# TensorE's steps of a beat placed ahead of the products of the beat's picks

## The chip, the cores and the metric

One core of a Trainium2 chip. The time is the device time of one execution in microseconds. The kernel before took 3504.87 us in the median of three runs (3503.13 to 3510.0).

## What is computed

One inference step of a single decoder layer, for a prompt of 1024 rows and eight sample sequences of four rows each behind 1024 cached positions, all in float32:

```python
h = rmsnorm(x, norm1_g)
p = h @ w_in                              # conv 512 | rwkv 1408 | attention 1152 columns
x = x + concat[conv_mixer(p), rwkv_mixer(p), sb_attention(q, k, v)] @ w_out
x = x + peer(rmsnorm(x, norm2_g))
y = rmsnorm(x, final_g)
```

`sb_attention` is a causal attention whose weights are the exponential of a log-sigmoid plus a running sum over later keys (stick-breaking). `rwkv_mixer` has a recurrence over the rows, done here in chunks of 64. `peer` is the costly part: for each row and each of 8 heads it scores 128 + 128 keys, takes the 16 best sums of pairs and with them 16 of 16384 experts, and then

```python
act = gelu(einsum('thkd,td->thk', u_tab[e], xb))
out = einsum('thk,thkd->td', gate * act, v_tab[e])
```

so every row fetches 8 x 16 rows of `u` and as many of `v`, 1024 floats each.

## The kernel before

The program has stages (`project`, `scan_rwkv`, `finish_rwkv`) and then `peer`, which begins near 600 us and holds all that the change touches. Rows are worked in nine blocks of 128 (`NBLK`; the ninth holds the 32 sample rows). A block has 8 turns, one for each head (`PH`; the ninth has 2), and a turn has 16 picks (`TOPK`), done in 8 groups of two (`GROUPS`, `GP`). A group is a *beat*; a full block has 64 of them, 512 in all with steps beside the picks, and 16 more in the ninth block.

The life of pick m:

- POOL (L1336) gathers, by the expert numbers of the turn, one row of `u` and `v` for each of the 128 partitions, 1 MB, into slot m mod 7 of `uv_ring` (`RING` is 7). Before it, it waits for `uv_free` to reach m - 6: the products of pick m - 7 are done.
- VectorE (L1769) waits for the gather and multiplies the `u` half with `h2`, summing to one number per row (`hidden`).
- ScalarE takes the gelu of both picks of the group (L1985), multiplies by the gate (L1989) and writes a diagonal matrix (`diag`, L1996; six of them, `DIAGS`).
- TensorE waits for `diag_done` and multiplies the diagonal with the `v` half, in four products that add to the banks `Y` (L2464), and raises `uv_free`.

Behind the picks of a group each engine does its part of the beat's other work. On VectorE this is gates, a piece of the choice of experts two turns ahead (`choose`, on odd beats), and `beside`. On ScalarE it is `exps` and `beside`. On TensorE it was the scores of a head three turns ahead (`score`, in the fifth beat of a turn), the spread of the final gain (`final_gain`, once a block) and `beside`. On POOL it is the fetch of a page of cached keys or values, now and then.

`beside(b, n)` is the same frame on every engine (`beats`): by the block and the number of the beat it calls what is due there, by tables written out by hand (`scans`, `finishes`, `early_seq`, `late_att`, and the constants `CLOSE`, `SPREAD`, `TURN`, `LATE`, `EARLY`):

- `attend`: attention of a later block in units of four tiles. Unit u has its scores in beat 2u (TensorE, L2371), logits in 2u + 2 (VectorE, L1672), softplus in 2u + 2 (ScalarE) and 2u + 3 (VectorE, L1684), sums over later keys in 2u + 3 (TensorE, L2385 and L2387), differences in 2u + 5 (VectorE), weights in 2u + 6 (ScalarE, L1935), values in 2u + 6 (TensorE, L2402). Scores wait for the logits of the unit before.
- `scan`: one chunk of the recurrence in 16 beats. Step n of TensorE (L2144) needs what VectorE (L1509 to L1526) or ScalarE (L1857 to L1863) makes in step n out of TensorE's step n - 1. There are 13 such chunks in the loop.
- `sample`: the attention of one sample sequence over its cached pages, in 22 beats, page by page (L2096, L2121); `scan_sample`: the recurrence of the samples, in the seventh block; `finish`: the group norm of the recurrence (L2351, L2354).
- closing of the next block: eight products with rows of `w_out` in beats 24 to 31 (`close_y`, L2056), residual and norm in beats 33 to 38 (`close_gain`, L2077, and `close_turn`, L2085, on TensorE).

Each engine runs its own program in order; only semaphores join them. SP loads what `beside` reads, waiting for counters that TensorE's steps raise. `beside` on TensorE waits for results of VectorE and ScalarE by semaphores as, in a scan:

```python
if n == 6:
    evicted("vr2")
    each("r3", lambda i, r: mm(lo(0)[r, i, :], p2[r, PR + i, :], rb[r, i, :]))
```

where `evicted("vr2")` waits until VectorE has written `r2` of this chunk, which it does in its own step 6.

Of the kernel before, what the change touches and what calls it, by code (L numbers as in the profile page):

```python
# [943 lines left out]
def peer(nc, io, sb):  # L944
# [11 lines left out]
    last = lambda b: b == NBLK - 1  # L956
    rows_of = lambda b: NS if last(b) else P
    GROUPS = TOPK // GP
# [76 lines left out]
    with ExitStack() as ctx:  # L1035
# [125 lines left out]
        def beats(b, n, attend, sample, scan, scan_sample, finish):  # L1161

            for block, c, first, rate in scans(b):
                for step in range(rate * (n - first), rate * (n - first) + rate):
                    if step in range(16):
                        scan(block, c, step)
            if b == S_TURN and n - S_SCAN in range(0, 2 * S_STEPS, 2):
                scan_sample((n - S_SCAN) // 2)
            for block, first in finishes(b):
                if n - first in range(5):  # L1170
                    finish(block, n - first)
            if b == 0:
                attend(1, n)
            if b and b + 1 < ATTENDED:
                attend(b + 1, n + BEATS - LATE)
            if early_seq(b) is not None:
                sample(early_seq(b), n - EARLY)
            if late_seq(b) is not None:
                sample(late_seq(b), n - LATE)
            if late_att(b) is not None:  # L1180
                attend(late_att(b), n - LATE)
# [824 lines left out]
        def _(pe):  # L2006
            def score(t):
                b, h = divmod(t, PH)
                if h == 0:
                    pe.wait_ge(KA.sem, KA.at("t1", b))  # L2010
                if t:
                    pe.wait_ge(C.sem, C.at("left1", t - 1))
                for c in range(DC):
                    if last(b):
                        for g in range(GR):
                            mine, head = slice(g * NS, (g + 1) * NS), h * GR + g
                            ins = nc.tensor.matmul(scores[mine, :], h2t[:, c, mine], wk[:, c, head * HN:(head + 1) * HN],
                                                   start=c == 0, stop=c == DC - 1)
                    else:
                        ins = nc.tensor.matmul(scores[:, :], h2t[:, c, :], wk[:, c, h * HN:(h + 1) * HN],  # L2020
                                               start=c == 0, stop=c == DC - 1)
                ins.then_inc(score_done, 1)

            def close_y(b, n):

                c = CLOSED_IN[n] if b else n
                if n == 0:
                    if b == 0:
                        for k in range(2):
                            pe.wait_ge(sb.wk_kept[k], PH * 2)  # L2030
                    if 0 < b < ATTENDED:
                        pe.wait_ge(logit_done, unit_at(b + 1, 0))
                        pe.wait_ge(diff_done, unit_at(b + 1, 0))
                    pe.wait_ge(mix_in, 16 * (b + 1 + (GR - 1) * last(b)))
                    if b >= 2:
                        pe.wait_ge(y_ready, b - 1)
                    if b:
                        pe.wait_ge(KA.sem, KA.at("t1", b - 1))
                if c >= DC - PA:
                    if last(b):  # L2040
                        pe.wait_ge(copied, GR)
                    else:
                        pe.wait_ge(out_kept, b + 1)
                if CT <= c < CT + PR:
                    if b:
                        pe.wait_ge(FV.sem, FV.at("gated", b - FRONT))
                    else:
                        pe.wait_ge(first_in, 16)
                recurrent = s_mixed if last(b) else ykept[:, b % 2, :, :]
                left = mixb[:, c, :] if c < CT else recurrent[:, c - CT, :] if c < CT + PR else att[:, c - (CT + PR), :]  # L2050
                if b == 0 and c in (0, len(STREAMED)):
                    pe.wait_ge(wo_in[c != 0], 16)
                if b and c in STREAMED:
                    pe.wait_ge(streamed, 16 * ((b - 1) * len(STREAMED) + c + 1))
                for k in range(2):
                    ins = nc.tensor.matmul(CB(b)[k][:, :], left[:, :], wo_of(b, c)[:, k * 512:(k + 1) * 512], start=n == 0, stop=n == DC - 1)  # L2056
                ins.then_inc(wo_used, 1)

            def final_gain(b):

                if b + 2 < ATTENDED:
                    pe.wait_ge(logit_done, unit_at(b + 3, 0))
                    pe.wait_ge(diff_done, unit_at(b + 3, 0))
                if b + 1 < NBLK and early_seq(b + 1) is not None:
                    pe.wait_ge(SV.sem, SV.at("diff", early_seq(b + 1)))
                pe.wait_ge(KA.sem, KA.at("t1", min(b + 1, NBLK - 1)))
                pe.wait_ge(gain_in, 16)
                for c in range(DC):
                    ins = nc.tensor.matmul(B[c // 4][:, c % 4 * P:(c % 4 + 1) * P], ident[HT:HT + DC, HT + c:HT + c + 1].to_broadcast([DC, P]), gain3,
                                           start=True, stop=True)  # L2070
                ins.then_inc(gain_spread, 1)

            def close_gain(b):

                pe.wait_ge(KV.sem, KV.at("x1", b))
                for c in range(DC):
                    ins = nc.tensor.matmul(B[c // 4][:, c % 4 * P:(c % 4 + 1) * P], ident[0:DC, c:c + 1].to_broadcast([DC, P]), gain2,  # L2077
                                           start=True, stop=True)
                KE.did(ins, "gain")

            def close_turn(b):

                pe.wait_ge(KV.sem, KV.at("h2", b))
                for c in range(DC):
                    ins = nc.tensor.transpose(B[c // 4][:, c % 4 * P:(c % 4 + 1) * P], h2[:, b % 2, c * P:(c + 1) * P], ident[:, :])  # L2085
                KE.did(ins, "turn")
# [328 lines left out]
            def beside(b, n):  # L2415

                beats(b, n, attend, sample, scan, scan_sample, finish)
                if n - CLOSE in range(DC):
                    close_y(b + 1, n - CLOSE)
                if n == SPREAD:  # L2420
                    close_gain(b + 1)
                if n == TURN:
                    close_turn(b + 1)
# [25 lines left out]
            for t in range(TURNS):  # L2449
                b, h = divmod(t, PH)  # L2450
                if h == 0 and b:
                    pe.wait_ge(summed, 4 * b)
                for q in range(GROUPS):
                    for k in range(GP):
                        m = at_group(t, q) * GP + k
                        begin, end = h == 0 and q == 0 and k == 0, t == last_turn(b) and m + 1 == after(t)
                        pe.wait_ge(diag_done, m + 1)
                        if last(b):
                            for j in range(2):
                                ins = nc.tensor.matmul(Y[j][0:NS, :], diag[:, m % DIAGS, 0:NS],  # L2460
                                                       v_row(m, slice(0, P), slice(j * 512, (j + 1) * 512)), start=begin, stop=end)
                        else:
                            for r, j in ((0, 0), (1, 0), (0, 1), (1, 1)):
                                ins = nc.tensor.matmul(Y[r][rows[j], :], diag[rows[r], m % DIAGS, :],  # L2464
                                                       v_row(m, rows[r], slice(j * 512, (j + 1) * 512)), start=begin, stop=end)
                        ins.then_inc(uv_free, 1)
                    if scored(t, q) < TURNS:
                        score(scored(t, q))
                    if b and (h, q) == SPREAD_FINAL[last(b)]:
                        final_gain(b - 1)  # L2470
                    if not last(b):
                        beside(b, h * GROUPS + q)
            pe.wait_ge(y_ready, NBLK - 1)
            final_gain(NBLK - 1)

# [169 lines left out]
```

## Time and profile before

| | |
|---|---|
| median of three runs | 3504.87 us |
| the profiled execution | 3511.46 us |
| its span, first to last instruction | 3509.3 us |
| TensorE products busy | 2804.1 us, 80% |
| VectorE busy | 2522.2 us, 72% |
| ScalarE busy | 1435.5 us, 41% |
| POOL busy | 1371.8 us, 39% |
| mean granted clock of TensorE | 0.874 of full speed |

A busy time is a sum over instructions. The products' ends are modelled and overlap; so TensorE at 80% isn't at its peak. The DMA engines have a row of their own: the mean busy share of sixteen engines, where neighbouring packets may overlap a little, so that 1.01 means full. In the timeline rows below the columns are start, duration, engine, line, operation, result and operands, count, and in brackets the idle time ahead with what ended it.

### The profile page before, as it was taken

How to read it: one execution, taken by the hardware profiler on the slowest of the kernel's cores; microseconds unless marked ns; L12 is line 12 of the kernel's file. 1: busy time of each engine (PE TensorE's matmuls, PEld its weight loads, DVE VectorE, ACT ScalarE, POOL GpSimd, SP SyncE). 2: the span in 40 equal slices, each digit the busy share in tenths (PEclk: the TensorE clock that was granted, in tenths of full speed). 3: DMA queues.
4: the chain of work that ended last, by engine and by line, in shares of the span. 5: the costliest groups of instructions: out<-in, count | busy, mean ns of one | idle time of the engine just before them, and what ended most of it. 6: DMA issues, size and time to landing. Idle time of an engine off the chain costs nothing.

```text
span 3509.3 us, 53126 instructions
## 1 busy us (share of the span) xinstructions
PE 2804.1 (80%) x19302; PEld 1383.5 (39%) x19302; DVE 2522.2 (72%) x5894; ACT 1435.5 (41%) x3859; POOL 1371.8 (39%) x1199
## 2 busy tenths in 40 slices
PE   8999977777778767976797779787878787777657
PEld 4555565434344324432443334334433344323211
DVE  2477333878877877788778877887788777776774
ACT  2121122535533553356335633574357433333332
POOL 0000000443454345434543454345444545454452
PEclk9999988988879888889888888898989888878879
DMA  3122343999999999999999999999999999999998
GB/s 99 40 58 82 107 144 130 403 415 401 410 413 414 395 419 415 404 403 418 416 405 408 415 415 405 396 418 416 403 406 412 417 414 410 401 416 399 409 419 343
DMA packets 248373, 1237.82 MB, mean 353 GB/s; under 512 B 62816, under 2 KB 90384, under 8 KB 112560
## 3 DMA queue, kind: packets, MB, share of 16 engines
q0 software_dynamic: 160256, 1132.54, 79.0%
q1 hardware_dynamic: 87856, 101.90, 8.6%
q8 instruction: 152, 2.49, 0.3%
q14 instruction: 109, 0.89, 0.1%
HBM read 1210.82 MB, written 23.53 MB: 352 GB/s over the span
## 4 chain that ended last, share of the span: by engine, by line
DMA 30%; PE 22%; DVE 20%; ACT 7%; issue 5%; POOL 1%; ACTq 0%; SPq 0%; DVEq 0%; POOLq 0%
DMA uv_ring<-in_peer_uv,expert 30%; PE peer_y L2464 11%; DVE uv_ring L1769 9%; PE peer_s L2020 3%; PE beside L2056 2%; PE scan L2144 2%; ACT diag L1996 1%; ACT L1985 1%; DVE same L1380 1%; DVE same L1382 1%; DVE pick L1384 1%; POOL uv_ring L1336 1%; ACT weights L1989 1%; ACT gelu L1985 1%; ACT L1941 1%
## 5 line engine op out<-in xcount | busy, mean ns | idle before, releaser
L1336 POOL DMA_INDIRECT uv_ring<-in_peer_uv,expert x1056 | 1223.6, 1159 | 1631.3 <-PE peer_y L2464 1282.4
L2464 PE MATMUL peer_y<-uv_ring,diag 64*64 64x512 f32 x8192 | 1250.3, 735 | 574.8 <-ACT diag L1996 541.9
L1769 DVE CUSTOM_DVE_ANT_0 uv_ring<-uv_ring,p_h 128x1024 f32<-128x1024 f32 x1056 | 1270.3, 1222 | 469.7 <-DMA uv_ring<-in_peer_uv,expert 463.5
L2464 PEld LDWEIGHTS peer_y<-uv_ring,diag 64*64 64x64 f32 x8192 | 307.9, 153 | 1181.6 <-ACT diag L1996 795.5
L1985 ACT ACTIVATE gelu<-hidden 128x2 f32<-128x2 f32 x528 | 107.4, 203 | 1420.6 <-DVE hidden L1769 1419.4
L594 PE MATMUL proj<-mix,w_in_tile 128*128 128x512 f32 x672 | 296.7, 600 | 0.0
L1996 ACT ACTIVATE diag<-ident_halves,weights 128x64 f32<-128x64 f32 x1024 | 292.5, 332 | 0.0
L1989 ACT ACTIVATE weights<-gelu,p_gate 128x1 f32<-128x1 f32 x1056 | 254.1, 287 | 50.5 <-ACT gelu L1985 1.5
L2020 PE MATMUL peer_s<-wk,p_h2t 128*128 128x256 f32 x1024 | 252.4, 402 | 4.0 <-DVE cand L1361 4.0
L2020 PEld LDWEIGHTS peer_s<-wk,p_h2t 128*128 128x128 f32 x1024 | 199.9, 201 | 96.4 <-issue 46.2
L1985 ACT ACT_TABLE_LOAD x172 | 220.7, 1283 | 3.0
L594 PEld LDWEIGHTS proj<-mix,w_in_tile 128*128 128x128 f32 x672 | 127.3, 192 | 153.1 <-issue 151.2
L671 POOL COPY v_c<-prc 128x192 f32<-128x192 f32 x2 | 0.7, 338 | 353.8 <-POOLq L129 353.8
L2371 PE MATMUL beside<-att_units,pages_ring 64*128 64x128 f32 x432 | 82.4, 312 | 17.4 <-DMA pages_ring<-scratch_k_tiles 6.8
L273 ACT ACTIVATE prc<-proj 128x512 f32<-128x512 f32 x15 | 9.0, 598 | 202.8 <-PE proj_tails L594 202.8
L418 DVE TENSOR_TENSOR prc<-prc 128x1088 f32<-128x1088 f32 x11 | 14.2, 1290 | 105.1 <-ACT prc L278 105.1
L1941 ACT ACT_TABLE_LOAD x69 | 88.5, 1283 | 1.2
L2371 PEld LDWEIGHTS beside<-att_units,pages_ring 64*128 64x128 f32 x432 | 60.2, 198 | 69.0 <-issue 52.7
L1769 DVE DVE_READ_ACCUMULATOR2_ANT hidden<- 128x1 f32 x1056 | 86.0, 81 | 0.0
L1790 ACT ACT_TABLE_LOAD x65 | 83.4, 1283 | 1.1
L1318 POOL DMA_INDIRECT pages_ring<-in_cache_v,page_rows x64 | 70.9, 1108 | 19.5 <-issue 17.1
L1318 POOL DMA_INDIRECT pages_ring<-in_cache_k,page_rows x64 | 70.6, 1103 | 19.5 <-issue 19.5
(453 smaller groups left out, 3746.3 us busy)
## 6 DMA issues: line engine op xcount, KB each, us to landing
uv_ring<-in_peer_uv,expert POOLq DMA_INDIRECT x1056
w_in_tile<-in_w_in SPq DMA_DIRECT2D x24, 512.0 KB, 3.3
w_out_rows<-in_w_out SPq DMA_DIRECT2D x24, 512.0 KB
uv_ring<-in_w_query SPq DMA_DIRECT2D x8, 1024.0 KB, 7.0
scan_in<-scratch_scan_in SPq DMA_DIRECT2D x15, 480.0 KB, 8.5
pages_ring<-scratch_k_tiles SPq DMA_DIRECT2D x36, 192.0 KB, 12.5
pages_ring<-out_v_new SPq DMA_DIRECT2D x36, 192.0 KB, 11.4
p_x<-in_x_rows SPq DMA_DIRECT2D x9, 512.0 KB, 8.7
```

What stands on the lines that cost most here:

```text
L594: last = nc.tensor.matmul(out, w[:, i % 3, c, :], h[:, c, lo:lo + size], start=c == 0, stop=c == DC - 1)
L1318: pool.indirect_dma_start(out=page[:, slot_of[what], :], out_offset=None, in_=io["cache_v" if kind else "cache_k"], in_offset=bass.Indirec ...
L1336: pool.indirect_dma_start(out=uv_row(m), out_offset=None, in_=io["peer_uv"], in_offset=bass.IndirectOffsetOnAxis(ap=expert[:, t % 4, k:k + ...
L1769: nc.vector.tensor_tensor_reduce(out=u_row(m), in0=u_row(m), in1=h2[:, b % 2, :], scale=1.0, scalar=0.0, op0=ALU.mult, op1=ALU.add, accum_ ...
L1790: nc.scalar.activation(expo[:, :], top[:, :], ACT.Exp, bias=neg[:, 0:1], accum_out=esum[:, 0:1]).then_inc(exps_done, 1)
L1941: nc.scalar.preload_act_table_set("natural_log_exp_and_others")
L1985: nc.scalar.activation(gel[:, g % 2, :], hid[:, g % 2, :], ACT.Gelu_apprx_tanh).then_inc(gelu_done, 1)
L1989: nc.scalar.activation(wgt[:, g % 2, k:k + 1], gel[:, g % 2, k:k + 1], ACT.Copy, scale=gate[:, t % 4, q * GP + k:q * GP + k + 1]).then_inc ...
L1996: nc.scalar.activation(diag[:, m % DIAGS, 0:n], eye[:, 0:n], ACT.Copy, scale=wgt[:, g % 2, k:k + 1]).then_inc(diag_done, 1)
L2020: ins = nc.tensor.matmul(scores[:, :], h2t[:, c, :], wk[:, c, h * HN:(h + 1) * HN], start=c == 0, stop=c == DC - 1)
L2371: ins = nc.tensor.matmul(B[0][:, i * P:(i + 1) * P], page[rows[e], k_slot(kt), h // 2 * P:(h // 2 + 1) * P], q_block[rows[e], h // 2, :], ...
L2464: ins = nc.tensor.matmul(Y[r][rows[j], :], diag[rows[r], m % DIAGS, :], v_row(m, rows[r], slice(j * 512, (j + 1) * 512)), start=begin, sto ...
```

## The change

In each beat of the first eight blocks TensorE calls `beside` ahead of the two picks' products instead of behind them and behind `score` and `final_gain`. The other engines' programs, all waits and all data stay as they are.

```diff
@@ -2451,6 +2451,8 @@
                 if h == 0 and b:
                     pe.wait_ge(summed, 4 * b)
                 for q in range(GROUPS):
+                    if not last(b):
+                        beside(b, h * GROUPS + q)
                     for k in range(GP):
                         m = at_group(t, q) * GP + k
                         begin, end = h == 0 and q == 0 and k == 0, t == last_turn(b) and m + 1 == after(t)
@@ -2468,8 +2470,6 @@
                         score(scored(t, q))
                     if b and (h, q) == SPREAD_FINAL[last(b)]:
                         final_gain(b - 1)
-                    if not last(b):
-                        beside(b, h * GROUPS + q)
             pe.wait_ge(y_ready, NBLK - 1)
             final_gain(NBLK - 1)
```

## Rows read from the trace of the kernel before

**Rows 1.** The page: DMA share in 40 slices, and the two large queues.

```profile
DMA  3122343999999999999999999999999999999998
...
q0 software_dynamic: 160256, 1132.54, 79.0%
q1 hardware_dynamic: 87856, 101.90, 8.6%
```

**Rows 2.** Stretches (busy by engine, clock, DMA share, GB/s), and the products' group.

```profile
644.00:3417.00 2773.00, 2163.08 (x16265) 1034.53 (x16268) 2167.84 (x5323) 1262.02 (x3460) 1320.84 (x1142) 0.86 1.01 410
1430.00:1450.00 20.00, 18.00 (x219) 11.86 (x219) 14.87 (x35) 8.01 (x23) 9.02 (x8) 0.98 0.93 356
1462.00:1484.00 22.00, 22.00 (x157) 10.28 (x160) 15.09 (x38) 5.19 (x22) 8.37 (x8) 1.00 1.01 419
...
L2464 PE MATMUL peer_y<-uv_ring,diag 64*64 64x512 f32 x8112 | 1237.2, 734 | 567.2 <-ACT diag L1996 534.3 <-DVE p_x L1407 31.6
```

**Rows 3.** The chain that ended last, by line.

```profile
DMA uv_ring<-in_peer_uv,expert 30%; PE peer_y L2464 11%; DVE uv_ring L1769 9%; PE peer_s L2020 3%; PE beside L2056 2%; PE scan L2144 2%; ACT diag L1996 1%; ACT L1985 1%; DVE same L1380 1%; DVE same L1382 1%; DVE pick L1384 1%; POOL uv_ring L1336 1%; ACT weights L1989 1%; ACT gelu L1985 1%; ACT L1941 1%
```

**Rows 4.** Waits: who waited for whom, us, times, longest.

```profile
POOL uv_ring L1336 <- PE peer_y L2464: 1282.4, 563, 8.1
...
PE peer_y L2464 <- ACT diag L1996: 541.9, 286, 6.7
DVE uv_ring L1769 <- DMA uv_ring<-in_peer_uv,expert: 463.5, 406, 3.6
...
ACT scan_y L1857 <- PE scan L2144: 28.0, 11, 3.1
```

**Rows 5.** The gathers: issue on POOL (ns, min/median/max) and landing.

```profile
L1336 POOL DMA_INDIRECT uv_ring<-in_peer_uv,expert x1056: 932/945/2000, 607.1 to 3484.6; - x176
...
DMA to landing us min/median/max: 4.9/7.0/12.5
```

**Rows 6.** Timeline 1350 to 1357 us: a scan step fed by VectorE, odd beat.

```profile
1351.34 1.95 PE L2464 MATMUL peer_y<-uv_ring,diag 64*64 64x512 f32 x16
...
1353.73 1.40 DVE L1526 TENSOR_TENSOR ra<-scan,p_ident 64x64 f32<-64x64 f32 x6
...
1355.19 0.56 PE L2144 MATMUL scan<-ra,p 64*64 64x64 f32 x12 [1.90 <-DVE ra L1526]
...
1355.68 0.84 PE L2096 MATMUL beside<-q_diag,pages_ring 128*128 128x8 f32 x6
```

**Rows 7.** Timeline 1370 to 1376 us: a scan step fed by ScalarE.

```profile
1372.02 1.95 PE L2464 MATMUL peer_y<-uv_ring,diag 64*64 64x512 f32 x16 [1.90 <-ACT diag L1996]
1372.11 0.31 ACT L1857 ACTIVATE p<-scan 128x192 f32<-128x192 f32 x1
...
1373.79 0.53 PE L2144 MATMUL scan<-p,xl 64*64 64x64 f32 x12
1374.24 0.83 PE L2096 MATMUL beside<-q_diag,pages_ring 128*128 128x8 f32 x6
```

**Rows 8.** Timeline 1578 to 1587 us: attention, an even beat.

```profile
1581.95 1.95 PE L2464 MATMUL peer_y<-uv_ring,diag 64*64 64x512 f32 x16 [0.42 <-ACT diag L1996]
...
1583.45 0.63 ACT L1935 ACTIVATE att_units<-att_units 128x512 f32<-128x512 f32 x1
1583.83 1.47 PE L2371 MATMUL beside<-att_units,pages_ring 64*128 64x128 f32 x8
...
1585.23 0.66 PE L2402 MATMUL beside<-att_units,pages_ring 128*64 128x128 f32 x8
```

**Rows 9.** Timeline 1595 to 1602 us: attention, an odd beat.

```profile
1597.62 1.95 PE L2464 MATMUL peer_y<-uv_ring,diag 64*64 64x512 f32 x16
...
1598.81 0.68 DVE L1684 SCALAR_TENSOR_TENSOR att_units<-att_units 128x512 f32<-128x512 f32 x1
...
1599.55 1.12 PE L2385 MATMUL beside<-att_units,s_tri 128*128 128x512 f32 x2
1600.52 1.02 PE L2387 MATMUL beside<-att_units,s_ones 128*128 128x512 f32 x2
```

## The prediction

> **What bounds the kernel now.** I read the slices of the page first, then the stretches, the chain, the waits, and last the order of time around single beats. The slices show the DMA engines at nine tenths from the moment the expert stage begins (about 620 us) to the end, and nearly all of what they move comes through the gathers of POOL's queue: 1132.54 MB against 101.90 MB [rows 1]. The stretches are sharper than the tenths: over 644 to 3417 us the DMA share is 1.01 at 410 GB/s, while TensorE is busy 2163 of 2773 us and VectorE 2168 [rows 2]. So the stage lasts as long as its bytes need, and the change moves no byte. A hole in the DMA is rare: 1430 to 1450 us, where the share is 0.93 and 20 us moved at 356 GB/s, is one, around a beat in which VectorE waited for TensorE; the stretch 1462 to 1484 us, in which closing products and picks alternate, is full (1.01) [rows 2]. The chain agrees: 30% of the span is a gather in flight, 11% are the products of the picks [rows 3].
>
> The waits show how close the rest follows. The ring has seven slots, so POOL may issue the gather of pick m only when the products of pick m - 7 are done; POOL waited 1282 us for just that, 563 times. VectorE waited for a gather at 406 of 1056 dots, 463.5 us in all. TensorE waited 541.9 us for a diagonal [rows 4]. It is one closed loop: gather, dot, gelu and diagonal, products, next gather; 2773 us for 8112 / 8 = 1014 picks [rows 2] is 2.73 us a pick, so one turn of the loop takes 7 x 2.73 = 19.1 us, 3.5 beats of 5.47 us.
>
> **The cushion.** A gather issue takes POOL 0.945 us, and a gather lands 7.0 us after it in the median, 4.9 us at least [rows 5]. The 2.1 us between are queueing behind other gathers. That is the cushion: products that end later by less than it leave the DMA engines full. A pick that has landed and waits for VectorE adds to it: at 650 of the 1056 dots VectorE did not wait for the gather.
>
> **The change, part by part.** Nothing is removed or added: the same instructions, waits and bytes. Between the products of beat n - 1 and those of beat n TensorE now does the steps of beat n where it did those of beat n - 1. TensorE's amount of work between two groups of products is the same, so that costs nothing by itself. Score and final_gain keep their place directly behind the products. No DMA is issued by TensorE. SP's and POOL's orders stay; their loads and page fetches that wait for TensorE's steps (wo_used, z_done, k_used, v_used, "state") are released one group of products earlier or, where the step itself waits, later by what is counted below. I cost that at nothing: those loads are asked for several beats ahead, and POOL stands waiting for products anyway; without that cover a page (about one gather issue, 0.945 us) would come on top at 128 page fetches.
>
> What it does add is exposure to waits. VectorE and ScalarE still do their part of beat n behind their share of the picks of beat n. Many steps of TensorE need what those two make in the same beat. Until now TensorE waited for it with the products already done; now the products of beat n are queued behind that wait, and behind them uv_free, the diagonals (six deep) and POOL. Four kinds, each from one beat:
>
> Scan step fed by VectorE on an odd beat. VectorE's choice of the next experts stands ahead of its step, which finishes at 1353.73 + 1.40 = 1355.13; TensorE's steps then take until about 1356.5; the products (1.95 us) would end near 1358.5 and ended at 1353.3: 5.2 us later [rows 6].
>
> Scan step fed by ScalarE. The copy ends at 1372.42, TensorE's steps take 1.3 us, products would end at 1375.7 and ended at 1373.97: 1.7 us [rows 7].
>
> Attention, even beat. The scores (1.47 us) can go at once; the values need the weights, ready at 1584.08, and take 0.66 us; the products would end at 1586.7, not 1583.9: 2.8 us [rows 8].
>
> Attention, odd beat. The suffix products need the softplus, ready at 1599.49; they take 2.0 us; 1603.4, not 1599.57: 3.9 us [rows 9].
>
> Counting in the code: the loop holds 13 scans of 14 dependent steps. Seven of the 14 are fed by ScalarE (91 beats x 1.7 = 155 us); of VectorE's seven about four fall on odd beats (52 x 5.2 = 270 us) and three on even ones, where by the code no choice stands ahead and only TensorE's 0.6 us step [rows 6] is in front of the products (39 x 0.6 = 23 us). There are 54 units of attention, each with one even and one odd beat (151 + 211 us). The samples' three waits in each of eight sequences, the closing turn, the finish and the sample scan come to some 100 us more. Closing products (beats 24 to 31) need nothing of the same beat. In all about 910 us of lateness in 512 beats, 1.8 us a beat. Some of it was there already, since TensorE was sometimes behind; I take 1.5 us a beat. That is under the cushion of 2.1 us, so on the average the DMA engines stay full; but 106 beats are late by 3.9 to 5.2 us and are not covered.
>
> The sum: a pick meets a product once in 3.5 beats. 106 / 3.5 = 30 turns with 4.5 - 2.1 = 2.4 us too much are 73 us; 54 / 3.5 = 15 turns with 2.8 - 2.1 = 0.7 are 11 us. Of these 84 us only that part bites in which the dot was really waiting for its gather, 406 / 1056 = 0.38: 32 us. What is given back: steps that come one group earlier take away VectorE's and ScalarE's waits for TensorE (28.0 us at ScalarE's scan_y [rows 4], and their like), but with the DMA full these are worth only their holes: 7% of 20 us, 1.4 us once a block, some 7 us. Net +25 us.
>
> Unknown prices, bounded. Share of the 84 us that bites: none of it (the landed picks cover everything) to all of it; I take 0.38, by the row of the waits. If nothing at all cushioned, 146 turns x 1.5 us would be +220 us; that is the far bound. Gain: at most the holes, which I put at 15 us at the outside, twice what I count.
>
> What the rows say of waiting for a gather is that its issue is tied to the products. The Trainium skill's page "DMA: Bandwidth & Descriptors" (Rules for kernel authors) says to issue a DMA early, do compute, and wait on its semaphore late. The change does the reverse, since POOL's issue hangs on the products; by that rule alone it would come out as rival C below. The rows alone bear it out only as far as the cushion is short.
>
> **The rivals.** Time of the profiled run: 3511.46 us, its span 3509.3, 2.2 us around it. The median of the runs is 3504.87, 6.6 below. The sum is a difference on that span (3511.5 + 25 = 3536) and I give it on the median: 3530.
>
> A, the forecast: the cushion covers most, odd beats break through. +8 to +75 us. Chance 0.50.
>
> B, the cushion holds altogether: the DMA engines stay at 1.01 and the time at 3505 +- 7. For it: 2.1 us of queueing and the 650 landed picks against 1.5 us of mean lateness. Against it: beats with 5.2 us follow each other at every second beat within a scan. Chance 0.24. The stretches show the DMA engines as the fullest resource in this stage. The Trainium skill's page "Perfetto Trace Analysis" (Identifying the Most-Contended Engine) says that a kernel generally improves by improving its most-contended engine; by that, an order on TensorE leaves 3505.
>
> C, the loop itself becomes the bound: lateness of one beat reaches VectorE's part of the next and so feeds itself, and the cushion is used up for good. Then from 84 us up to 220 us: 3590 to 3725. It decides once the mean lateness exceeds 2.1 us. For it: 1.8 us before my deduction. Against: VectorE's own step ends sooner where it waited for TensorE. Chance 0.16.
>
> D, faster: the products of the closing beats and the gain and turn steps are what makes VectorE late around beats 21 and 35 of a block (the hole of 1430 to 1450 us), and having them a group sooner fills the holes, with the cushion holding elsewhere. Price 8 to 15 us: 3490 to 3497. It needs the holes to be worth more than all uncovered lateness. Chance 0.10.
>
> That the change does nothing at all is excluded: two thirds of the beats have a step.
>
> **Numbers.** 0.2% is 7 us, about what a measurement of this kernel can tell from no change. Faster is D, same is B, slower is A and C. The range goes from 3496 (most of D left out) to 3600 (A whole, the low end of C); about two in ten stay outside.
>
> **What would show it.** Right: POOL's wait for the products grows well over 1282 us; TensorE's wait for diagonals falls from 541.9 us and in its place stand waits of the scan, of L2385 and L2402 for VectorE and ScalarE, several hundred us in all; gathers land nearer to 4.9 us than to 7.0; DMA share 0.98 to 1.00 and GB/s near 406 in blocks 1 to 5, and the last two blocks (no scans, little attention) unchanged. VectorE's waits for the gather rise over 463.5 us. Wrong: a DMA share of 1.01 throughout with an unchanged time (B), a landing median at 5 us and blocks longer by over 10 us each (C), or waits for products that shrink.

## The result, and the profile after

The changed kernel takes 3667.36 us in the median against 3506.44 us for the kernel before on the same chip, a ratio of 1.0457 (95% interval 1.0421 to 1.0494): about 160 us slower. The forecast was 3530, with a range up to 3600. The measured time falls into the band of rival C, 3590 to 3725, to which I had given 0.16; whether C's mechanism is what happened is another matter, taken up below. The profiled execution took 3662.16 us, its span 3660.4.

The stretches of the changed kernel, by block and last the stage between the same beats as [rows 2]; columns as there (the last two are DMA share and GB/s):

```profile
978.00:1345.00 367.00, 274.71 (x2108) 136.09 (x2108) 274.58 (x673) 157.65 (x436) 162.10 (x144) 0.86 0.98 390
1345.00:1725.00 380.00, 289.27 (x2140) 145.02 (x2140) 278.41 (x686) 167.45 (x450) 159.01 (x145) 0.83 0.96 381
...
3227.00:3571.00 344.00, 235.06 (x1420) 90.29 (x1420) 247.43 (x605) 117.55 (x380) 170.00 (x144) 0.80 0.99 408
...
644.00:3565.00 2921.00, 2200.61 (x16230) 1071.55 (x16222) 2175.37 (x5313) 1255.92 (x3452) 1289.06 (x1141) 0.85 0.97 388
```

Where [rows 2] had 2773 us at 410 GB/s and a share of 1.01, there are now 2921 us at 388 GB/s and 0.97. The bytes are the same; the DMA engines run dry again and again, in every block that has recurrence, attention or the samples' recurrence, and hardly in the eighth, which has only one sample sequence and a group norm (344 us, share 0.99). The seventh, at 2853 to 3227 us, has no chunk of the prompt's recurrence and still took 374 us where it had taken 353. All of the loss is in this stage: 148 us of the profiled spans' 151.

The waits of the changed kernel, as in [rows 4] (L2466 is the old L2464):

```profile
POOL uv_ring L1336 <- PE peer_y L2466: 1445.5, 507, 14.9
DVE uv_ring L1769 <- DMA uv_ring<-in_peer_uv,expert: 675.1, 512, 5.5
...
PE peer_y L2466 <- ACT diag L1996: 190.9, 92, 5.4
...
PE beside L2385 <- DVE att_units L1684: 81.6, 29, 6.5
...
PE scan L2144 <- DVE xd L1509: 56.4, 20, 6.1
...
PE scan L2144 <- ACT p L1857: 49.2, 21, 5.0
...
PE beside L2402 <- ACT att_units L1935: 39.7, 26, 5.3
...
PE scan L2144 <- ACT scan_in L1857: 32.2, 14, 4.5
PE scan L2144 <- DVE arb L1518: 31.5, 10, 6.9
```

TensorE's wait for diagonals fell from 541.9 to 190.9 us, and in its place stand waits inside its other steps for what VectorE and ScalarE make in the same beat. Summed over all such rows (not shown one by one), TensorE's steps other than the products waited for those two engines 79 us before and 531 us now. POOL's wait for products rose from 1282.4 to 1445.5 us with its longest from 8.1 to 14.9 us, and VectorE's wait for gathers from 463.5 to 675.1.

One beat shows the mechanism: the same scan step as in [rows 6], in the changed kernel. Timelines of TensorE, VectorE, ScalarE and POOL:

```profile
1382.24 1.95 PE L2466 MATMUL peer_y<-uv_ring,diag 64*64 64x512 f32 x16
1388.94 0.91 PE L2144 MATMUL scan<-ra,p 64*64 64x64 f32 x12 [4.75 <-DVE ra L1526]
1389.78 1.45 PE L2096 MATMUL beside<-q_diag,pages_ring 128*128 128x8 f32 x6
1391.15 3.48 PE L2466 MATMUL peer_y<-uv_ring,diag 64*64 64x512 f32 x16
...
1383.90 0.17 DVE L1375 TENSOR_SCALAR pos_part<-pos 128x16 uint32<-128x16 uint32 x1
...
1387.49 1.40 DVE L1526 TENSOR_TENSOR ra<-scan,p_ident 64x64 f32<-64x64 f32 x6
...
1384.70 0.57 ACT L1996 ACTIVATE diag<-ident_halves,weights 128x64 f32<-128x64 f32 x2
...
1385.19 1.05 POOL L1336 DMA_INDIRECT uv_ring<-in_peer_uv,expert  x1 [0.31 <-issue]
1393.44 1.68 POOL L1336 DMA_INDIRECT uv_ring<-in_peer_uv,expert  x1 [7.21 <-PE peer_y L2466]
```

VectorE ends the dots at 1383.98 (the first line of VectorE here starts the choice) and the diagonal is ready near 1385.0, but TensorE waits until `ra` is written at 1388.9, behind the whole choice, then does its steps, and starts the products at 1391.15. [rows 6] had them 0.05 us behind the diagonal. POOL, which had nothing else to issue, stands for 7.21 us. The DMA engines feel it some microseconds on: over 1384 to 1400 us their share is 0.89, and over 1394 to 1395 us alone it is 0.20.

### The profile page after: what moved, and what is told of

It is laid out like the page before. It is cut to its first block, busy times and chain, and to the rows that moved or that the text cites. A ratio compares the mean times of both kernels' runs of the same rounds, so it can differ in the third digit from the quotient of the medians.

```text
span 3660.4 us, 53123 instructions
## 1 busy us (share of the span) xinstructions
PE 2844.6 (78%) x19302; PEld 1422.5 (39%) x19302; DVE 2532.7 (69%) x5894; ACT 1432.9 (39%) x3859; POOL 1343.6 (37%) x1199
## 4 chain that ended last, share of the span: by engine, by line
DMA 33%; PE 26%; DVE 17%; issue 4%; ACT 3%; POOL 2%; SPq 0%; DVEq 0%; ACTq 0%; POOLq 0%
DMA uv_ring<-in_peer_uv,expert 33%; PE peer_y L2466 11%; DVE uv_ring L1769 6%; PE scan L2144 3%; PE beside L2056 2%; POOL uv_ring L1336 2%; PE peer_s L2020 1%; DVE same L1382 1%; DVE same L1380 1%; DVE pick L1384 1%; PE beside L2385 1%; PE beside L2371 1%; ACT diag L1996 1%; PE beside L2387 1%; PE beside L2077 1%
## 5 line engine op out<-in xcount | busy, mean ns | idle before, releaser
L1336 POOL DMA_INDIRECT uv_ring<-in_peer_uv,expert x1056 | 1191.7, 1129 | 1810.8 <-PE peer_y L2466 1445.5
L1769 DVE CUSTOM_DVE_ANT_0 uv_ring<-uv_ring,p_h 128x1024 f32<-128x1024 f32 x1056 | 1277.8, 1224 | 682.5 <-DMA uv_ring<-in_peer_uv,expert 675.1
L2466 PE MATMUL peer_y<-uv_ring,diag 64*64 64x512 f32 x8192 | 1213.7, 714 | 215.1 <-ACT diag L1996 190.9
L2466 PEld LDWEIGHTS peer_y<-uv_ring,diag 64*64 64x64 f32 x8192 | 323.0, 154 | 809.8 <-issue 443.5
L2385 PE MATMUL beside<-att_units,s_tri 128*128 128x512 f32 (+1 forms) x112 | 75.7, 764 | 110.9 <-DVE att_units L1684 81.6
```

What stands on the lines that cost most here:

```text
L1336: pool.indirect_dma_start(out=uv_row(m), out_offset=None, in_=io["peer_uv"], in_offset=bass.IndirectOffsetOnAxis(ap=expert[:, t % 4, k:k + ...
L1769: nc.vector.tensor_tensor_reduce(out=u_row(m), in0=u_row(m), in1=h2[:, b % 2, :], scale=1.0, scalar=0.0, op0=ALU.mult, op1=ALU.add, accum_ ...
L2385: ins = nc.tensor.matmul(B[1][:, 0:k * P], tri[:, :], soft[:, n % 2, 0:k * P], start=True, stop=not older, skip_group_check=True)
```

## The experiments

All times below are differences against the kernel before, run beside each experiment on the same chip: the ratio less one, times 3506 us. The interval of the ratio stands in brackets.

### Which steps cost: recurrence, attention, closing, the rest

In three kernels one kind of TensorE's steps goes ahead of the products and the others stay behind, by a switch:

```diff
+            def beside(b, n, ahead):
+                part = lambda name, f: f if (name in AHEAD_OF) == ahead else none
+                beats(b, n, part("attend", attend), part("sample", sample), part("scan", scan), part("scan", scan_sample), part("finish", finish))
                 for q in range(GROUPS):
+                    if not last(b):
+                        beside(b, h * GROUPS + q, True)
                     for k in range(GP):
...
+                    if not last(b):
+                        beside(b, h * GROUPS + q, False)
```

Recurrence alone:

> TensorE's steps of the two recurrences alone go ahead of the products; attention, samples, finish and closing stay behind. Head-of-line theory (products queue behind waits for what VectorE and ScalarE make in the same beat, and the closed loop of seven slots gets longer): 13 chunks of 14 dependent steps are about half of the lateness, so +60 to +90 us over before, all of it in blocks 0 to 5. Rival (any TensorE work that stands right ahead of the products costs its own time): the recurrence is some 15% of that work, so about +25 us.

Measured: 1.0103 (1.0086 to 1.0119), +36 us. Attention alone:

> Only the prompt's attention goes ahead. Head-of-line theory: 54 units with a wait in each of their two beats, +50 to +80 us. Rival (work, not waits): attention is some 35% of TensorE's work beside the picks, about +55 us. This run alone doesn't part them; with the other two of the set it does, as the sum of the parts is to come near +161 us.

Measured: 1.0207 (1.0189 to 1.0224), +73 us. The closing products and the spread of the gain alone:

> Only the closing products and the spread of the gain go ahead, about 20 us of TensorE's time in each block, none of which needs anything of the same beat. Head-of-line theory: no change, 0 to -8 us, and POOL's wait for products as before. Rival (work, not waits): these are the longest steps of all, 2.3 us a beat ahead of the products in nine beats of eight blocks, +20 to +40 us.

Measured: 1.0012 (1.0003 to 1.0022), +4 us, at most 8. Nine long steps a block stand right ahead of the products and cost next to nothing, where the rival (any work of TensorE ahead of the products costs its own time) had +20 to +40 us. Attention fits the waits, but it fits the rival as well, as was said before it ran. Recurrence costs less than the waits led me to expect (+60 to +90 us) and lies nearer to the rival's 25; it doesn't decide between the two. Here are its waits (this is the recurrence kernel, in which attention still stands behind):

```profile
PE scan L2144 <- DVE xd L1509: 58.2, 21, 5.8
...
PE scan L2144 <- ACT p L1857: 43.3, 21, 4.5
PE scan L2144 <- DVE ra L1526: 35.0, 10, 5.0
```

The waits of the recurrence are all there, as long as in the changed kernel, and still only 36 us come through. How late a product is and what it costs are two things: there is some room in the loop. Then the part left over, and two together:

> The part not tried yet: samples' attention, the group norm's two products and the closing transposes go ahead, all else behind. The parts measured so far are +36 (recurrence), +75 (attention) and +4 us (closing), 115 of 161. If the parts add up, this one is worth the missing +46 us. If lateness only costs once it has used up the room in the loop, the parts tried one by one look smaller than together, and this one gives under +25 us.

Measured: 1.0098 (1.0074 to 1.0122), +34 us, between the two values that I had named (46, and under 25). Its largest wait is the samples' suffix sums, a chain of small VectorE operations, once in each of eight sequences:

```profile
PE beside L2109 <- DVE att_units L1474: 50.5, 8, 8.2
```

> Recurrence and attention together go ahead, samples, finish and closing stay behind. If their costs add up: +111 us. If lateness costs more where some is there already (the room in the loop is used once): +125 us or more. The rival that parts share one room and overlap would give under +100 us.

Measured: 1.0251 (1.0228 to 1.0274), +88 us, under the sum of 109, so those two overlap a little. All four parts tried singly sum to 36 + 73 + 4 + 34 = 147 us against 160 together, which is near; but the near sum hides two deviations. Samples and closing cost 34 + 4 = 38 us alone and 160 - 88 = 72 us on top of the other two. So the parts share room and also add to one another, and only in the sum does it come out even. An edge below which lateness is free doesn't show in any of them.

### How much room the loop has

```diff
-RING = 7
+RING = 6
```

> The kernel before, with a ring of six slots and not seven: the same loop with one pick of 2.73 us less room, which measures the cushion by itself. With the cushion of 2.1 us that the prediction took, only 0.6 us of each turn of the loop would show, up to +90 us. If it is near 1 us, some 1.7 us of each turn shows, +200 to +290 us. If the DMA engines alone set the time and the loop has much room, under +20 us.

Measured on the kernel before: 1.0386 (1.0365 to 1.0406), +135 us. One turn of the loop is seven picks, so 1024 / 7 = 146 turns; 135 / 146 = 0.9 us of each 2.73 us came through. My cushion of 2.1 us would have allowed at most 90 us, so it is wrong; 1.8 us of the 2.73 were absorbed on the average. The same on the changed kernel:

> The changed kernel with a ring of six. In the kernel before the seventh slot was worth 141 us, half of the 2.73 us a turn, as the rest fell into room. If the change has used up the room, a slot less now costs nearly its whole 1/7: over +250 us on the changed kernel's 3667 us, 3900 us or more. If room is still left, it is worth about +141 us again, 3800 us.

Measured: 1.1189 (1.1127 to 1.125) against the kernel before, +417 us, thus 257 us on top of the changed kernel's 160. The seventh slot is worth 1.9 times as much as before the change, so the change had used up part of the room. Both as stretches of about the same 1014 picks; first the kernel before with six slots, then the changed one with six:

```profile
644.00:3555.00 2911.00, 2197.51 (x16211) 1045.42 (x16210) 2169.67 (x5305) 1255.57 (x3445) 1295.91 (x1139) 0.84 0.98 389
```

```profile
644.00:3844.00 3200.00, 2286.32 (x16261) 1109.74 (x16255) 2188.18 (x5320) 1258.84 (x3456) 1264.78 (x1143) 0.82 0.91 355
```

The time of a turn follows: six picks at 2911 / 1014 us are 17.2 us before and six at 3200 / 1014 are 18.9 us changed. With seven it was 19.1 us before (DMA full) and 7 x 2921 / 1014 = 20.2 us changed. To hide a slot's loss altogether a turn has to get shorter by one pick. It got 1.9 us shorter of 2.7 in the kernel before, and 1.3 of 2.9 in the changed one: a third came through before the change and over a half after it. Seen the other way, with six slots the change made a turn 1.7 us longer, against some 1 us with seven. Note the first row beside the changed kernel's stage above: one slot less looks like the change, 389 and 388 GB/s, with shares 0.98 and 0.97.

### The place of TensorE's steps, or their order to the other engines

VectorE and ScalarE too do their steps ahead of the picks' work:

```diff
@@ vector, scalar
                     g = at_group(t, q)
+                    if not last(b):
+                        beside(b, h * GROUPS + q)
...
-                    if not last(b):
-                        beside(b, h * GROUPS + q)
```

> The changed kernel, and VectorE and ScalarE too do their steps beside the picks ahead of the dots and of the gelu of the beat. TensorE's steps stand as far ahead as in the changed kernel, and what they need of the same beat is made ahead of the picks as well. Head-of-line theory (what counts is the order of the engines to each other): back to the time before, within 15 us of it, and the lateness of the products behind their diagonal falls back to about 1 us. Rival (TensorE's steps ahead of the products cost by their place): it stays 100 us or more above before.

Measured: 1.0014 (1.0000 to 1.0028), +5 us. TensorE's program is the changed kernel's word for word, and the loss is gone. The stage is full again, and the wait is back on the diagonals, at what [rows 4] had:

```profile
644.00:3416.00 2772.00, 2153.04 (x16214) 1032.58 (x16213) 2164.79 (x5305) 1231.94 (x3427) 1308.88 (x1139) 0.86 1.00 409
...
PE peer_y L2466 <- ACT diag L1998: 550.5, 297, 6.2
```

So what counts is the order of the engines to each other, not where TensorE does its own steps.

### Which waits: the choice, odd and even beats

Only VectorE's choice and gates are moved behind its steps, in the changed kernel:

```diff
@@ vector
+                    if not last(b):
+                        beside(b, h * GROUPS + q)
                     if gated(t, q) < TURNS:
                         gates(gated(t, q))
...
-                    if not last(b):
-                        beside(b, h * GROUPS + q)
```

> The changed kernel, with VectorE doing its steps beside the picks directly behind the dots and its gates and choice of experts behind them. That takes only the choice (up to 3.4 us in the odd beats) out of what TensorE waits for; order and work are else the changed kernel's. Head-of-line theory with the choice as the large term: half of the 161 us or more is won back, 3590 us or less. If the waits for ScalarE and for VectorE's own steps are the larger part: 3620 us or more. If it is the place of TensorE's own work: 3667 us, unchanged.

Measured: 1.0235 (1.0189 to 1.0281), +82 us: half of the 160 is the choice (with the gates) standing ahead of what TensorE needs. What is left are ScalarE, whose steps are done behind the diagonals, and VectorE's own steps behind its dots, in about equal parts: TensorE's steps waited 223 us for the one and 208 for the other, where in the changed kernel it was 177 and 354. The largest of these waits:

```profile
PE beside L2402 <- ACT att_units L1935: 64.8, 40, 5.4
PE scan L2144 <- ACT scan_in L1857: 62.0, 27, 5.1
PE beside L2371 <- DVE att_units L1672: 50.8, 22, 5.7
```

TensorE's steps ahead in odd beats only, or in even beats only:

```diff
-                    if not last(b):
+                    if not last(b) and q % 2 == 1:
                         beside(b, h * GROUPS + q)
                     for k in range(GP):
...
+                    if not last(b) and q % 2 == 0:
+                        beside(b, h * GROUPS + q)
```

> TensorE's steps go ahead of the products in the odd beats of a turn only, in which VectorE's choice stands ahead of its own step; in even beats they stay behind. The prediction said that the odd beats (3.9 to 5.2 us late) do nearly all the harm and the even ones are covered: then +110 us or more here and under +40 us for the even ones. If lateness costs wherever it falls, both give +60 to +110 us. Rival: two beats' steps now stand in one gap, and the clump itself costs; then both are alike and together above 161 us.

Measured: 1.0445 (1.0413 to 1.0476), +156 us.

> The same with the even beats: under +40 us if only the long waits of the odd beats break through, +60 to +110 us if lateness costs wherever it falls. In attention's even beats TensorE waits for ScalarE's weights, 1.3 us of table load and 0.6 us of work behind the diagonals.

Measured: 1.024 (1.0215 to 1.0266), +84 us. Odd beats weigh about twice as much as even ones, so the direction of my weighting stands; but the even ones aren't covered. The sum of 240 us is above 160, as the rival of a clump said, by which two beats' steps in one gap cost by themselves; how they do it was not tried. So these two runs rank odd over even and don't give either beat's share of the 160.

### Between the two products

```diff
                     for k in range(GP):
+                        if k == 1 and not last(b):
+                            beside(b, h * GROUPS + q)
```

> TensorE's steps of the beat stand between the products of its first and of its second pick. The first slot of each pair is freed as early as in the kernel before, the second as late as in the changed one. If the room in the loop counts slot by slot, about half of the cost: +60 to +100 us. If the later slot of the pair alone sets the pace, +130 us or more. If what matters is that POOL always has one gather to issue early, under +40 us.

Measured: 1.0167 (1.0146 to 1.0188), +59 us, just below the 60 to 100 of "slot by slot". One slot of each pair is freed nearly on time and the other late, and a bit over a third of the loss is left. The later slot of a pair doesn't set the pace alone.

### How much of the lateness comes through

The traces give the lateness itself: for each of the 1024 picks of the full blocks, the time from the end of its diagonal on ScalarE to the start of its products on TensorE. Its mean is 1.29 us in the kernel before and 3.60 us in the changed one. Added lateness times the 146 turns of the loop, against what each kernel cost:

| TensorE's steps ahead | added lateness, us | cost, us | share that came through |
|---|---|---|---|
| samples, finish, turn | 0.30 | 34 | 0.8 |
| recurrence | 0.69 | 36 | 0.4 |
| attention | 0.86 | 73 | 0.6 |
| even beats | 1.14 | 84 | 0.5 |
| between the two products | 1.17 | 59 | 0.3 |
| all, choice behind | 1.56 | 82 | 0.4 |
| recurrence and attention | 1.58 | 88 | 0.4 |
| odd beats | 1.80 | 156 | 0.6 |
| all (the change) | 2.31 | 160 | 0.5 |

The two kernels without a loss, closing ahead and all engines ahead, have no added lateness (-0.15 and -0.04 us). The costs have the intervals given above, so that the 0.8 may be 0.6 to 1.0; the lateness is that of one profiled execution. No run shows a mean lateness that is free, and no single factor holds either; why the shares differ stays open.

Where the rest goes is seen in the parts of one turn of a slot, as means over the picks issued behind 644 us. The landing is the slot's last DMA record ahead of its next issue:

| us | before | changed | six slots | changed, six slots |
|---|---|---|---|---|
| issue of the gather to its landing | 10.8 | 9.7 | 9.3 | 8.8 |
| landed, until VectorE starts the dot | 1.4 | 1.0 | 1.1 | 0.6 |
| start of the dot to end of the diagonal | 3.6 | 3.6 | 3.6 | 3.6 |
| diagonal to start of the products (lateness) | 1.3 | 3.6 | 1.2 | 3.7 |
| products | 1.3 | 1.3 | 1.3 | 1.3 |
| products to the slot's next issue | 0.8 | 1.0 | 0.7 | 0.9 |
| one turn | 19.2 | 20.2 | 17.3 | 18.9 |

The change put 2.3 us into a turn. The gathers landed 1.1 us sooner, as fewer of them were in flight at a time, and waited 0.4 us less for VectorE; POOL's next issue came 0.2 us later behind the products. In all 1.0 us came through, and 146 turns of it are about 150 us, the loss of the stage.

No kernel tried is faster than the kernel before: the nearest two are 4 and 5 us above it, and both run at a DMA share of 1.00 to 1.01.

## Why the prediction was wrong

What it had right: the bound (a full DMA, whose bytes the change leaves alone); the mechanism (products queued behind waits for the same beat, uv_free late, POOL late); where (the blocks with scans and attention most, the eighth hardly); and the exchange of waits. The closing beats cost nothing, as it said. That the last two blocks stay unchanged was right of the eighth only (344 us against 338); the seventh lost 21 us. I had counted some 100 us of lateness for the samples, the turn and the finish together; the traces add 147 us in the beats with samples' steps alone. POOL's page fetches, costed at nothing, did cost nothing; POOL waited 1.5 us there for TensorE's steps before and 1.8 us now. The sign was right. The size was wrong by a factor of six, in three steps.

**The cushion.** "A gather lands 7.0 us after it in the median, 4.9 us at least. The 2.1 us between are queueing behind other gathers. That is the cushion." This is the step that failed, twice over.

First, it misread the row. [rows 5] calls the landing times those of the gathers; they belong to the ten loads of weights that SP puts into `uv_ring` at 450 to 533 us, ahead of this stage. The page of the kernel before has a landing time for those and none for the gathers, which the page of the kernel with the closing steps ahead has:

```profile
uv_ring<-in_peer_uv,expert POOLq DMA_INDIRECT x1056
uv_ring<-in_w_query SPq DMA_DIRECT2D x8, 1024.0 KB, 7.0
```

```profile
uv_ring<-in_peer_uv,expert POOLq DMA_INDIRECT x1056, 11.0
```

Worked out from the DMA records of each slot, a gather of the kernel before landed 10.8 us behind its issue in the median and 5.9 us at least. With these numbers the same reasoning gives a cushion of 4.9 us, more than the 2.73 us of a whole slot and than every lateness in the sum but the 5.2 us, and so no loss to speak of. That the forecast named a loss at all is in part luck, owed to a number that measured something else.

Second, and this is the fault of the step itself: queueing is no edge below which lateness is free. The kernel before with six slots lost 135 us, where 4.9 us of such a cushion would have hidden all of it. In the changed kernel the gathers still landed 9.8 us behind their issue in the median, 4.4 us above its fastest, and the DMA share was 0.97 all the same: much queueing is left on the average while at moments there is none, as at 1394 us in the beat shown. The sign of being right, gathers that land sooner, did appear (10.8 to 9.8 us in the median), but not near 4.9 us.

**The mean lateness.** I summed 1.8 us and took 1.5 us a beat, "since TensorE was sometimes behind". From the first diagonal's end to the first product's start, over 512 beats, the mean went from 0.85 to 3.16 us: 2.3 us more, as over all picks. So the deduction for beats already behind was the wrong way. By kinds of beat, with the difference of the two kernels' traces: attention was counted rightly (2.8 us in even beats and 3.9 in odd ones, both as worked out), and so were the odd beats of a scan (3.2 us; 5.2 and 1.7 in my count, according to who feeds the step). The even beats of a scan were 2.8 us later where I had 0.6 to 1.7, and the 105 beats with neither scan nor attention nor samples 0.4 to 0.5 us later where I had next to none. That lateness is handed on from one beat to the next would do this, but no run tried it by itself. In the beat shown the products began 6.1 us behind the diagonal, where I had worked out 5.2 later in all, as TensorE had stood idle 4.75 us and then its steps took 2.2 us (1388.94 to 1391.15) and not 1.3, and the products 3.48 us and not 1.95.

**What comes through.** 146 turns x 2.3 us are 337 us, and 160 came through: 0.47 of all lateness. I had let only the excess over 2.1 us count, and of it 0.38: 32 us. Counted with the same 146 turns, the runs with less lateness than 2.1 us let 0.3 to 0.8 of it through, down to an added 0.3 us that cost 34 us. The second factor, the share of dots that waited for their gather, takes it that all other gathers have room; the landed gathers waited 1.4 us for VectorE on the average before and 1.0 us in the changed kernel, so that room gave 0.4 us and no more.

Of the gains, 7 us for filled holes, nothing shows. VectorE's and ScalarE's waits for TensorE did get shorter (ScalarE's `scan_y`, 28.0 us in [rows 4], is down to 5.5), but VectorE then waits longer for gathers. The Trainium skill's rule on issuing a DMA early and waiting late ("DMA: Bandwidth & Descriptors", Rules for kernel authors) pointed to rival C and was borne out: POOL's wait for products is up by 163 us, the time by 160. The Trainium skill's rule to optimize the most-contended engine first ("Perfetto Trace Analysis", Identifying the Most-Contended Engine), read as "an order on TensorE changes nothing while the DMA is full", did not hold: the order decides whether the DMA stays full.

That the time fell into rival C's band doesn't make C right. Its condition ("once the mean lateness exceeds 2.1 us") was met, at 2.3, but 2.1 came from the misread row, and the runs show no switch: parts of the change with 0.3 to 1.8 us of lateness cost 34 to 156 us. What C had right is the absence of a reserve that covers it all. That the loop feeds its own lateness "for good" isn't shown.

## What to carry to other kernels

Where an engine works off a queue in order, put the work that frees a buffer ahead of any step that waits for another engine's part of the same round; if steps are moved ahead on one engine, move their makers ahead on the others too. A full DMA says that the engines beside it cost nothing now, not how much later they may get: measure that room by taking one buffer away, and count lateness as a share of all of it (here 0.3 to 0.8), never as free up to an edge read from a landing time. And when a row gives a time for a buffer, see which transfers it covers: the loads that fill it once at the start and the gathers that fill it 1056 times are both under its name.

## What the runs showed of the hardware that I had not expected

TensorE's clock enters through the wait. Behind the 4.75 us of idleness from 1384.2 us on, the granted clock was 0.50, the level of 1.2 GHz, from 1389 to 1394 us, and the sixteen product instructions took 3.48 us and not 1.95. Over the 16 us it was 0.79, a mix of that level and 2.4 GHz:

```profile
1384.00:1400.00 16.00, 11.25 (x102) 6.54 (x102) 13.03 (x39) 6.45 (x19) 7.27 (x7) 0.79 0.89 344
```

Over the whole stage it is no term: the clock is 0.85 against 0.86 in [rows 2], and the products of a beat took 2.4 us in the mean in both kernels.

The time from issue to landing of a gather of this size, 1 MB in rows of 8 KB, follows how many are on the way. It was 10.8 us in the median in the kernel before, 9.8 in the changed one, 9.3 with six slots and 8.8 with six slots and the change; the mean time divided by the time of a pick gives 3.9, 3.4, 3.2 and 2.8 gathers in flight. The fastest took 5 to 6 us in all four.
